# A fused decoder-layer kernel: part of the sample attention's start moves into the prompt mixers, and its last three jobs change order

## The reference, cut to what matters

```
u = rmsnorm(x, g_mix)
proj = jnp.einsum('btd,df->btf', u, w_in)
...
o_cmp = jnp.einsum('bgjti,bigd->btgjd', p_cmp.astype(q.dtype), vcmp)
imp = jnp.einsum('bgjti,is->bgts', p_cmp, cmp_to_sel(n_cmp, n_sel))
...
imp = jnp.where((jj == 0) | (jj == q_pos[:, None] // SEL_BLOCK), FORCE_SCORE, imp)
_, idx = lax.top_k(imp, min(SEL_TOP, n_sel))
o_sel = sel_attend(qg, ksb, vsb, idx.astype(jnp.int32), q_pos)
o_win = window_attend(qg, win_kv[:, :, 0], win_kv[:, :, 1], kw_pos, q_pos)
o = g[..., 0:1] * o_cmp + g[..., 1:2] * o_sel + g[..., 2:3] * o_win
```

## Time and profile before

| | before |
|---|---|
| three runs | 1584.5, 1579.6, 1583.37 us (median 1583.37) |
| profiled execution | 1580.48 us, its span 1578.7 us |
| mean granted clock of PE | 0.942 of full speed |
| busy share of the span | PE 91%, DVE 55%, ACT 25%, POOL 5% |
| 185 to 425 us | PE busy 232.62 of 240 us, granted clock 0.99 |
| 425 to 756 us | PE busy 272.30 of 331 us, clock 0.86 |
| 756 to 884 us | PE busy 84.97 of 128 us, clock 0.79 |

### The profile page before, as it was taken

The page is one execution under the profiler, slowest core; times in us unless marked ns, Lnnn a source line. Parts: engine busy times, 40 slices in busy tenths (PEclk is TensorE's granted clock), DMA queues, the critical chain, the costliest instruction groups (busy, mean ns, idle before and its releaser), DMA issues. The chain is left out here.

```text
span 1578.7 us, 27041 instructions
## 1 busy us (share of the span) xinstructions
PE 1433.3 (91%) x11344; PEld 1319.4 (84%) x11344; DVE 865.6 (55%) x1569; ACT 390.6 (25%) x896; POOL 82.0 (5%) x76
## 2 busy tenths in 40 slices
PE   5999999899887886889657799999899999999998
PEld 5888889899877775768444698999799999999998
DVE  3566257777463566554424535556647646465563
ACT  3543032332352444443223410000022001010000
POOL 1000001100010111111100000000000000000000
PEclk9999999999987798979778899999899999999999
DMA  9232124222331000010666523333421232322321
GB/s 362 71 141 88 52 78 177 76 81 85 119 139 54 0 2 1 1 54 1 227 267 222 185 80 94 108 94 94 161 79 56 81 108 81 103 84 88 99 81 55
DMA packets 115648, 159.03 MB, mean 101 GB/s; under 512 B 6039, under 2 KB 106839, under 8 KB 112778
## 3 DMA queue, kind: packets, MB, share of 16 engines
q1 hardware_dynamic: 111886, 122.76, 24.2%
q0 software_dynamic: 2304, 33.56, 5.3%
q10 hardware_dynamic: 1348, 1.12, 0.2%
HBM read 145.04 MB, written 16.66 MB: 102 GB/s over the span
## 5 line engine op out<-in xcount | busy, mean ns | idle before, releaser
L330 PE MATMUL ps<-hH,wh 128*128 128x260 f32 x512 | 145.8, 285 | 2.6 <-DVE hT L301 2.6
L330 PE MATMUL ps<-mergedH,wh 128*128 128x260 f32 x512 | 145.8, 285 | 0.0
L330 PE MATMUL ps<-hT,wh 128*128 128x260 f32 x512 | 145.6, 284 | 0.0
L330 PE MATMUL ps<-hH,wl 128*128 128x260 f32 x512 | 145.3, 284 | 0.0
L330 PE MATMUL ps<-mergedT,wh 128*128 128x260 f32 x512 | 145.0, 283 | 0.0
L330 PE MATMUL ps<-mergedH,wl 128*128 128x260 f32 x512 | 144.7, 283 | 0.0
L330 PE MATMUL ps<-uH,wh 128*128 128x260 f32 x480 | 137.8, 287 | 0.0
L462 PE MATMUL ps<-XT,w 128*128 128x256 f32 (+1 forms) x512 | 124.7, 386 | 0.3 <-DVE hbias L615 0.3
L330 PE MATMUL ps<-uL,wh 128*128 128x260 f32 x384 | 109.0, 284 | 0.0
L330 PE MATMUL ps<-uH,tw 128*128 128x260 f32 x384 | 109.0, 284 | 0.0
L462 PEld LDWEIGHTS ps<-XT,w 128*128 128x128 f32 x512 | 93.6, 194 | 11.3 <-issue 0.9
(11 more groups left out here) (548 smaller groups left out, 3563.8 us busy)
## 6 DMA issues: line engine op xcount, KB each, us to landing
wt<-in_w_ff SPq DMA_DIRECT2D x32, 1024.0 KB, 5.4
wt<-in_w_in SPq DMA_DIRECT2D x15, 1024.0 KB, 5.3
tw<-in_w_in SPq DMA_DIRECT2D x12, 1024.0 KB, 5.3
ring<-in_cache_mem_kv SPq DMA_DIRECT2D x4, 2048.0 KB, 11.6
w<-in_cmp_w SPq DMA_DIRECT2D x8, 512.0 KB, 7.8
ring<-in_cache_win_kv SPq DMA_DIRECT2D x2, 2048.0 KB, 9.6
out_s_win<-in_cache_win_kv SPq DMA_DIRECT2D x1, 4088.0 KB
scratch_uhigh<-uH SPq DMA_DIRECT2D x1, 2080.0 KB
```

Source lines behind the costliest of these rows:

```text
L330: ins = pe.matmul(out, lhsT(i, c), rhs(j, c), start=(first and c == 0 and k == 0), stop=(last and c == chunks - 1 and k == 2))
```

## The change

Three parts. In `stage_inputs` the turns of "m" and "mem" get later keys. In `stage_prompt_mixers` the pairs are laid a little closer (1.2 becomes 1.17), the last step's gain and gate go from POOL to DVE, the sample's compressed chain comes in as `top_pe`, `top_act` and `top_dve` (for both halves in one instruction where that can be), and four instead of two gathers are issued; the choice of the best 16 stays at the start of the next stage. In `stage_sample_attention` that chain is gone, and half 1 has its win job ahead of its sel job: piece 7 is the window, pieces 8 to 11 are gathers.

```
-        base = {"mem": end("mem") + 0.5, "q": end("q") + 0.5, "m": end("m") + 0.5, "k": end("k") + 0.5}
+        base = {"mem": end("mem") + 0.5, "q": end("q") + 0.5, "m": end("m") + 5.0, "k": end("k") + 0.5}
...
-        key_side = lambda g, t: key_tile(g, t + 1) + 0.8
+        key_side = lambda g, t: key_tile(g, t + 1) + (3.2 if g == "mem" else 0.8)
...
+        if t == TT - 1:
+            z = self.proj[:, t, tok_col(C_Z):tok_col(C_Z) + GH * GD].rearrange("p (h d) -> p h d", d=GD)
+            yield key(t, 12) + 0.06
+            ch.step(dve.tensor_tensor(sq[:, 0:GH, :], sq[:, 0:GH, :], heads(self.V("gdn_o_norm")), ALU.mult))
+            ch.step(dve.tensor_tensor(z, z, sq[:, 0:GH, :], ALU.mult))
...
-        self.ring_filled = 2
+        self.ring_filled = 4
...
-                n = length or (2.6 + 0.65 * tiles_of(min(u, hi - 1))) * 1.2
+                n = length or (2.6 + 0.65 * tiles_of(min(u, hi - 1))) * 1.17
...
+        top_key = lambda k: self.delta_key(TT - 1, 12) + (-3.0, -1.0, 0.03, 0.09)[k]
...
+            def top_pe(pe):
+                both = range(NB // 4)
+                yield top_key(0)
+                pe.wait_ge(p_ready, 2 * NU)
+                pe.wait_ge(o_done, NU)
+                for r in both:
+                    for j in range(4):
+                        ins = pe.matmul(ps[32 * j:32 * j + 32, 0, P * r:P * r + NCMP], self.qblk[:, 4 * r + j, :], self.kcT[:, 4 * r + j, 0:NCMP], start=True, stop=True)
+                ins.then_inc(c_s, 1)
+                yield top_key(1)
+                pe.wait_ge(c_chain, 2)
+                for r in both:
+                    ins = pe.transpose(ps[0:NCMP, 1, P * r:P * r + P], top["pc"][:, r, 0:NCMP], ident)
+                ins.then_inc(c_pt, 1)
...
+            def top_dve(dve):
+                s, two = top["cst"], lambda i: ps[:, i, 0:2 * P].rearrange("p (r n) -> p r n", r=2)
+                yield top_key(0)
+                dve.wait_ge(c_s, 1)
+                dve.tensor_reduce(s[:, 0, :], two(0)[:, :, 0:NCMP], AX, ALU.max, negate=True).then_inc(c_max, 1)
+                yield top_key(1)
+                dve.wait_ge(c_exp, 2)
+                dve.reciprocal(s[:, 2, :], s[:, 1, :]).then_inc(c_chain, 1)
...
+                yield top_key(2)
+                dve.wait_ge(c_imp, 1)
+                dve.tensor_copy(top["imps"][:, :, 0:NSEL], two(2)[:, :, 0:NSEL]).then_inc(c_impk, 1)
+                dve.wait_ge(c_o, 1)
+                dve.tensor_copy(top["out"], two(3)).then_inc(c_chain, 1)
...
+                yield 50.0
+                pool.wait_ge(o_done, MU)
+                pool.wait_ge(gates, TT + 2)
+                self.gather_piece(pool, 2, 2)
                 yield self.delta_key(TT - 1, 2.5)
                 self.d_pe.wait(pool, "tv", TT - 1)
                 self.d_dve.wait(pool, "sc", TT - 1)
                 self.gather_piece(pool, 1, 1)
+                yield self.delta_key(TT - 1, 11.9)
+                pool.wait_ge(o_done, NU)
+                self.d_pe.wait(pool, f"Y{self.LEVELS - 1}", TT - 1)
+                self.gather_piece(pool, 3, 3)
...
-        jobs = [(br, r) for r in range(R4) for br in ("sel", "win", "mem")]
+        jobs = [("sel", 0), ("win", 0), ("mem", 0), ("win", 1), ("sel", 1), ("mem", 1)]
```

More of the change, by code:

```diff
@@ L1540, in stage_prompt_mixers @@
         self.delta_setup()
+        late = (self.taken["w1"][1], self.taken["mem_kv"][0])
+        assert late[1] - late[0] >= PAGES * 256
+        self.taken["ring3"] = late
+        self.ring.append(self.view("ring3", [P, PAGES * 256], F32))
+        self.top_setup()
+        top = self.top
         S = self.local_sem
         w_loaded = S("d_w")
+        c_s, c_max, c_exp, c_pt, c_ptk, c_imp, c_impk, c_o, c_chain = (S("e_c" + x) for x in (
+            "s", "max", "exp", "pt", "ptk", "imp", "impk", "o", "chain"))
         turned, kept, gelu, small_ready, small_kept = (S("d_" + x) for x in ("turned", "kept", "gelu", "small", "smallkept"))
@@ L1722, in cmp_act @@
                 yield 44.0
-                act.wait_ge(c_max, 1)
-                act.activation(sc[:, :, :, :, :], sc[:, :, :, :, :], ACT.Exp).then_inc(c_exp, 1)
+                act.wait_ge(d_max, 1)
+                act.activation(sc[:, :, :, :, :], sc[:, :, :, :, :], ACT.Exp).then_inc(d_exp, 1)
                 for qt in range(TT):
@@ L1893, in stage_prompt_mixers, with top_setup @@
         self.taken["ring1"] = (at, at + PAGES * 256)
+    def top_setup(self):
+        kv = lambda t, c, n: self.proj[:, t, C_KV + c:C_KV + c + n]
+        two = lambda x: x.rearrange("p (r n) -> p r n", r=2)
+        self.top = dict(pc=two(kv(0, 0, 2 * P)), PTc=two(kv(0, 2 * P, 2 * P)), imps=two(kv(1, 0, 4 * P)),
+                        imp=[kv(1, 2 * P * r, 4 * NSEL).rearrange("p (a n) -> p a n", a=4) for r in range(NB // 4)],
+                        out=kv(slice(0, 2), 4 * P, P), cst=kv(2, 4 * P, 8).rearrange("p (a r) -> p a r", r=2))
+        self.scr = {n: self.nc.dram_tensor("scratch_" + n, (NB, 32, w), F32, kind="Internal").ap()
+                    for n, w in (("cmp", P), ("sel", P), ("win", P), ("mem", 512))}
+        self.c_scr = self.sem("e_cscr")
     def gather_piece(self, pool, b, n):
@@ L1935, in stage_sample_attention @@
         self.tw0, self.u_back = self.view("tw0", [P, KC, WCOLS], F32), self.sem("t_u_back")
-        scr = {n: nc.dram_tensor("scratch_" + n, (NB, 32, w), F32, kind="Internal").ap()
-               for n, w in (("cmp", P), ("sel", P), ("win", P), ("mem", 512))}
-        jobs = [(br, r) for r in range(R4) for br in ("sel", "win", "mem")]
+        jobs = [("sel", 0), ("win", 0), ("mem", 0), ("win", 1), ("sel", 1), ("mem", 1)]
+        new_rows = [sum(x != "mem" for x, _ in jobs[0:n + 1]) for n in range(len(jobs))]
         NJ = len(jobs)
@@ L1973, in stage_sample_attention @@
         gathered, fetched = self.filled, [S(f"e_fetched{k}") for k in range(RING)]
-        c_s, c_max, c_exp, c_pt, c_ptk, c_imp, c_impk, c_o, c_chain, c_done = ([S(f"e{r}_" + x) for r in range(R4)] for x in (
-            "s", "max", "exp", "pt", "ptk", "imp", "impk", "o", "chain", "done"))
-        c_scr = S("e_cscr")
         turned, kept, s_done, s_read, nmax, p_ready, o_ready, o_read = (S("e_turned"), [S("e_kept0"), S("e_kept1")], S("e_scores"), S("e_sread"),
```

158 lines of the change are left out of this document (71 added, 87 removed).

## The result

The changed kernel takes 1597.64 us (median of 7 runs, 1587.69 to 1599.9) against 1583.37 us (median of 7 runs, 1579.6 to 1586.13). The ratio of their times is 1.0079, with a 95% interval of 1.0057 to 1.0101: 12.5 us slower. (The two medians lie 14.3 us apart; differences in time are given by the ratios from here on.) The direction was forecast, the size was not: 1587 us was predicted, within 1567 to 1595.

What follows compares the result with a forecast made beforehand. PE was the engine to watch, through its idle waits in three stages. Terms of -5.5 and +10.9 us summed to +5.4, 1585.9 on the profiled 1580.48; put on the four times' mean of 1582.0, 1587 us, range 1567 to 1595.

Steps and rivals of the forecast that it cites:

- Stage inputs, -5.5: In `stage_inputs`, later turns remove PE's 4.3 and 0.9 us waits for DVE's norming: 5.5 us less, ends 5 and 6.5.
- Stage prompt mixers, +1.0 between -1 and +3: End of `stage_prompt_mixers`: work moved onto DVE behind the last output puts the end at 757.8 instead of 756.84.
- the sum: All stage terms together: -5.5 + 10.9 = +5.4 us, of which 1.0 is the mixers' later end.
- The compressed chain and half 0, -8.7: Start of `stage_sample_attention`: third key turns 6.5 us sooner, 2.2 us gather wait gone; together 8.7, less 1.0 late start.
- The rival that the chain would hold delta's last step: End of mixers: o products stand behind a turn waiting for DVE and ACT, +3 us, 1590; chance 0.05.
- The window's wait, 18: Sample attention, half 1: window load takes packet turns with four gathers, lands at t0 + 29; PE waits about 18 us.
- Half 1 without waits, 59.1 + 2: Half 1's instructions take 59.1 us without gather waits, plus 2 for KT copies behind the sel job's softmax.
- The end of the stage, 22.4 us after the sel job: Sample attention's end: output write and reads held by the u reload; tail starts at 896.8 instead of 885.96, +10.9.
- the first (the window lands in time): Rival in half 1: bytes shared or window packets out early, window wait 0 to 2 us, sum -11.6, 1570; chance 0.27.

Runs made afterwards that it cites:

- b_keys: Kernel before with only the later keys of the "m" and "mem" turns in stage inputs: 1575.73 us, ratio 0.9964 to the kernel before.
- b_beat117: Kernel before with only the factor of the pairs' keys at 1.17 instead of 1.2: 1588.36 us, ratio 1.0048 to the kernel before.
- a_gather_late: Changed kernel, but POOL waits for the half 1 window to land before issuing half 1's first gather: 1589.05 us, ratio 1.0045 to the kernel before.
- a_old_jobs: Changed kernel with half 1's jobs back in the order sel, win, mem: 1569.0 us, ratio 0.9925 to the kernel before.
- o_gather2: Changed kernel with half 1's jobs in the old order and only two gathers issued in the mixers: 1580.98 us, ratio 0.999 to the kernel before.
- a_win_4k: Changed kernel with the window loaded in 4 KB runs, 512 packets instead of 2048: 1581.83 us, ratio 0.9991 to the kernel before.
- a_reads_first: Changed kernel with SP's reload of u issued behind the six output reads instead of ahead: 1593.07 us, ratio 1.0065 to the kernel before.

## Why the prediction was wrong, by its own steps

**Stage inputs, -5.5: right, a little large.** 4.45 us in the profile, 5.7 in b_keys. The wait at the first turn went as worked out; that DVE's weight split would stand ahead of the third tile was not seen, and costs 1.8 us.

**Stage prompt mixers, +1.0 between -1 and +3: this is the step that failed.** It measured +7.87 in the profile, the largest miss of the sum. The prediction said "the closer pairs (1.17) give nothing by themselves, since delta's chain sets this end". It costed the end of the stage, where it was right (4.16 us from L1493 to the next stage, 0.5 less than before), and put the re-spacing of 64 pairs at nothing without reading a row of the 250 us in which they run. b_beat117 prices the factor at 7.6 us. Less that, the changed kernel would stand some 4.9 us over the kernel before (12.5 less 7.6, an estimate), where the sum had 5.4. The delta chain does set the end, but it runs on the same PE as the pairs, and L1493 came 8.4 us later into the stage with PE at the lower clock. Why 1.17 has PE at the lower level for longer between 520 and 640 us is not settled. The level goes with the loss in most of the rows: 0.74 and 0.75 where the stage was slow, 0.82 to 0.89 where it was not; a_gather_late had 0.74 there too and took 330.1 us, so that stretch is not the whole of it. The stage also varies with the same program: 326.5, 330.1, 336.5, 336.9 and 337.0 us in five profiles with the same mixers code and the factor 1.17. The fastest of them is a_old_jobs:

```profile
424.81:751.31 326.50, 274.73 (x1999) 237.35 (x2000) 182.65 (x425) 140.73 (x333) 48.13 (x41) 0.88 0.13 47
```

The same products kept PE busy for 274.73 us at a clock of 0.88 and for 287.02 at 0.83. So in the changed kernel 1.17 does not always cost; one profile of a kernel can't price it, the 12 runs of b_beat117 can, on the kernel before. This variation may be most of the spread of the changed kernel's runs (12 us, at a mean clock of 0.930 to 0.941); only one of those runs has a trace.

**The compressed chain and half 0, -8.7: right.** 8.07. The rival that the chain would hold delta's last step is out: its turn (L1738, at 753.49) stands ahead of the first `o` product with 0.34 us of idle time before it, and `o` itself waited 0.23 us, for ACT. o_gather2 shows that the two early gathers carry the gain: without them v_done reaches 1 only 0.6 us sooner than in the kernel before.

**The window's wait, 18: right in the rule; that the size is right too is luck, since two errors of the sum cancel.** Measured 17.8. Turns by packet are shown by 552 packets beside 578, and by a_win_4k. By the rule of the Trainium skill ("DMA: Bandwidth & Descriptors", queues, rings and completion order) each engine takes its rows in turn, a packet at a time; the trace agrees. What I had left out is that the window's load starts about 4 us ahead of the gathers and moves half its bytes alone, so that it needed 2.7 us behind their end and not 8; what I had counted too short is the gathers, which start 4.8 us behind v_done = 1 and end near 26.2 and not 21.

**Half 1 without waits, 59.1 + 2: too small.** It took 64.8 (82.57 less 17.77). The missing 3.7 us are not the softmax in front of the KT copies, which I had put at 2: the wait of 3.3 us for L2285 is there in a_win_4k too, where the same work took 58.6. They are PE's lower clock, 0.50 to 0.89 in the changed kernel and 0.79 to 1.00 in a_win_4k, 6.2 us in all. That the long wait is its cause is only in part shown: a_gather_late, with three gather waits of at most 4.6 us in its place, had the low clock too and took 65.4.

**The end of the stage, 22.4 us after the sel job: right,** 23.0. The write lands late, the reads behind it, as worked out. a_reads_first moved the stall from the reads to the mem output's write, and to the reload's own end.

**The chances.** No rival came true. For the first (the window lands in time) the wait had to be 0 to 2 us; even with the 4 KB runs of a_win_4k it was 6.0. That the time came out slower, as forecast, rests on the order (+22 to +24 us), but at 1587 us it was forecast for a smaller sum than the one that came. What was missing is a rival in the mixers' middle, and the range (to 1595) had no room for one beside a full wait for the window. The account by the ratios: keys -5.7, factor +7.6, order +22 to +24, and by subtraction -11 to -14 for the chain with its gathers, the last known only to a few us and only if the factor costs in the changed kernel what it costs in the kernel before.

## What to carry to other kernels

A factor that re-spaces work over a whole stage can't be costed from the stage's end: time its middle, by PE's busy time and granted clock in windows, over several executions, or expect either sign. A load of small rows that is issued beside gathers in large packets got one packet for each of theirs here; give it longer runs, or issue it earlier or alone, and count what it moves before the others start. Before a job is moved later, look at what is hung on its end: here a 5 MB reload that lost two thirds of its cover, and held a write of 64 KB beside it for 10.5 us.

## What the runs showed of the hardware that was not expected

A 17.8 us idle stretch of PE was followed by 11.3 us at a granted clock of 0.50 and 21.0 at 0.89, where after 6.0 us idle the same work ran at 0.79 and 1.00. The first of several gathers moved its first packets 1.6 us after its issue with no load in front, and 4.5 us after it with a 2 MB load issued 0.2 us ahead on SP's queue. Moving the same 2 MB in 512 packets instead of 2048 beside four gathers took 11.8 us off its landing, while the gathers' own times changed little (16.9 instead of 16.4 us for the fourth). Five executions of the same mixers code lay 10.5 us apart at clocks of 0.83 to 0.88.
